# Two transformer blocks on one core: the first attention stage projects its tokens without their root mean square

## The reference, cut to what matters

```python
def rms_norm(x, g):
    y = xf * lax.rsqrt(jnp.mean(xf * xf, axis=-1, keepdims=True) + EPS)     # EPS = 1e-6
    return y * g

h = rms_norm(x, ln_mix[l]);  proj = h @ w_in[l]
q_g, k_g, v_g, q_lat, kv_lat = split(proj)                   # 512, 128, 128, 256, 128 + 32 columns
q_g = apply_rope(rms_norm(q_g per head of 64, gqa_q_norm));  k_g likewise
o_g = attention(q_g, k_g, v_g)                               # 8 heads of 64, 2 key/value heads
c_q = rms_norm(q_lat, mla_q_norm);  c_kv = rms_norm(kv_lat[:128], mla_kv_norm)
k_rope = apply_rope(kv_lat[128:])                            # shared by the 8 latent heads
o_m = attention(c_q @ w_q_b, [c_kv @ w_kv_b, k_rope], values from c_kv @ w_kv_b)
x = x + concat(rms_norm(o_g), rms_norm(o_m)) @ w_o
```

## Time and profile before

| | us |
|---|---|
| median of 3 runs | 3021.49 (3018.26 to 3021.59) |
| the profiled execution, its time | 3016.69 |
| its span, first to last instruction | 3014.9 |
| TensorE busy (matmuls) | 2821.8, 94% of the span |
| VectorE busy | 1422.9, 47% |
| ScalarE busy | 1127.0, 37% |
| GpSimd busy | 238.3, 8% |
| mean granted TensorE clock | 0.974 of full speed |

### The profile page before, as it was taken

How to read it: one execution, slowest core, us unless ns; L and a number is a source line. 1 busy time by engine, 2 the same in 40 slices (tenths; PEclk the granted TensorE clock), 3 DMA queues, 4 the chain that set the end, 5 groups by cost and what they waited for, 6 DMA issues and landing times.

```text
span 3014.9 us, 40098 instructions
## 1 busy us (share of the span) xinstructions
PE 2821.8 (94%) x16212; PEld 2099.0 (70%) x16212; DVE 1422.9 (47%) x2150; ACT 1127.0 (37%) x1917; POOL 238.3 (8%) x229
## 2 busy tenths in 40 slices
PE   7999979989999879999999799999999999799998
PEld 5657844537658744447877578888888787578886
DVE  6665532337666323244545763333334654753444
ACT  4664431124654411135233652222222542643332
POOL 0011020000011100001001010000001111000001
PEclk9999989999999989999999899999999999899999
DMA  4011249981002269983425112233220234222220
GB/s 156 29 43 68 88 175 418 417 356 52 28 29 100 113 254 419 418 354 140 145 99 162 33 72 112 112 120 132 112 84 24 82 120 128 82 84 98 98 98 28
DMA packets 67909, 428.28 MB, mean 142 GB/s; under 512 B 7968, under 2 KB 8352, under 8 KB 20368
## 3 DMA queue, kind: packets, MB, share of 16 engines
q1 hardware_dynamic: 62144, 407.96, 35.4%
q0 software_dynamic: 4432, 15.67, 1.6%
q10 hardware_dynamic: 1152, 2.10, 0.2%
HBM read 416.78 MB, written 8.91 MB: 141 GB/s over the span
## 4 chain that ended last, share of the span: by engine, by line
PE 81%; DVE 7%; ACT 4%; DMA 3%; issue 2%; POOL 2%; SPq 0%; DVEq 0%; ACTq 0%; POOLq 0%
PE banks L854 78%; PE banks L855 3%; ACT arena L1685 3%; DVE arena L2376 3%; DMA weight<-in_w_up 2%; POOL arena L3184 2%; DVE arena L3031 1%; DVE weight_part L2480 1%; ACT weight_part L1685 0%; DVE arena L2665 0%; DVE arena L2663 0%; DMA block_tokens_high<-df_stage 0%; DVE x L2376 0%; DMA weight<-in_ada_w 0%; POOL block_tokens_low L3198 0%
## 5 line engine op out<-in xcount | busy, mean ns | idle before, releaser
L1685 ACT ACTIVATE arena<-banks 128x512 f32<-128x512 f32 (+3 forms) x510 | 279.3, 550 | 876.5 <-PE banks L854 767.5
L854 PE MATMUL banks<-weight,arena 128*64 128x512 f32 (+4 forms) x2136 | 428.9, 573 | 19.1 <-ACT arena L1685 8.5
L854 PE MATMUL banks<-hidden,weight_part 128*128 128x512 f32 (+1 forms) x2304 | 446.8, 355 | 0.0
L854 PEld LDWEIGHTS banks<-hidden,weight_part 128*128 128x128 f32 x2304 | 381.1, 189 | 70.4 <-issue 3.8
L854 PE MATMUL banks<-tokens_high,weight_part 128*128 128x512 f32 (+1 forms) x1536 | 409.6, 358 | 10.0 <-ACT tokens_high L1685 10.0
L2480 DVE TENSOR_TENSOR weight_part<-weight,weight_part 128x2048 fp32r<-128x2048 f32 x124 | 285.6, 2306 | 199.7 <-ACT weight_part L1685 199.6
L1685 ACT ACTIVATE weight_part<-weight 128x2048 fp32r<-128x2048 f32 x124 | 236.4, 1908 | 361.2 <-PE banks L854 336.4
L854 PEld LDWEIGHTS banks<-weight,arena 128*64 128x64 f32 (+2 forms) x2136 | 150.8, 136 | 253.2 <-issue 231.5
L854 PEld LDWEIGHTS banks<-tokens_high,weight_part 128*128 128x128 f32 x1536 | 274.4, 191 | 62.6 <-DVE arena L2376 16.0
L3184 POOL TENSOR_TENSOR arena<-arena 128x512 f32<-128x512 f32 (+1 forms) x89 | 115.9, 1302 | 1978.0 <-ACT arena L1685 1711.4
L854 PE MATMUL banks<-tokens_low,weight_part 128*128 128x512 f32 (+1 forms) x768 | 264.7, 354 | 0.0
(11 more groups left out here) (216 smaller groups left out, 3886.4 us busy)
## 6 DMA issues: line engine op xcount, KB each, us to landing
weight<-in_w_gate SPq DMA_DIRECT2D x64, 1024.0 KB, 13.7
weight<-in_w_up SPq DMA_DIRECT2D x64, 1024.0 KB, 8.1
weight<-in_w_down SPq DMA_DIRECT2D x64, 1024.0 KB, 11.1
weight<-in_w_ff SPq DMA_DIRECT2D x64, 1024.0 KB, 4.8
weight<-in_ada_w SPq DMA_DIRECT2D x48, 1024.0 KB, 6.3
weight<-in_w_in SPq DMA_DIRECT2D x28, 1024.0 KB, 5.9
weight<-in_w_o SPq DMA_DIRECT2D x8, 1024.0 KB, 4.8
weight<-in_w_mem_kv SPq DMA_DIRECT2D x8, 1024.0 KB, 4.9
```

The source lines that it names most:

```text
L854: mm = lambda o, a, b, first=True, last=True: eng.matmul(o, a, b, start=first, stop=last, skip_group_check=True)
L1685: act = lambda o, i, f=ACT.Copy, **k: eng.activation(o, i, f, **k)
```

## The change

HH and HL are made from X * gain, without the root: `tokens_high` (ScalarE, Copy with the gain as scale) and `tokens_low` (VectorE, X * gain - HH). They no longer wait for the squares, which come behind HH in ScalarE's queue. `entry_sums` moves between the high and the low part of `joint3`. All outputs of the projection are now larger by the token's root mean square. Inner norms take that out by themselves, apart from their epsilon: a norm of c/r with EPS is a norm of c with EPS * r * r, r * r being the token's mean square plus EPS. So each sum of squares of g, cq and ckv gets one further matmul (`token_eps`: 64 rows, fp32r, high and low part) that adds EPS * (ms + EPS), and its root and Newton step take epsilon 0. What isn't normed later is scaled by the token's root YM: the values vt and the shared rotated key kr, both now a product on VectorE where ScalarE copied before. The root YM itself (Ln, Exp, Newton) is taken behind the splits of weight chunk 1. On TensorE each per-head sum comes one output later (sum t-2 and turn t-3 follow raw t), and turn 4 comes behind cq 1.

```diff
@@ -607,7 +607,10 @@
             b.update(paired(c, t, T, 4, (2, 2)))
-            b["SQW"] = Ring(st, "SQW" + t, [b["H"][:, k, :] for k in range(KD)])
+            b["SQW"] = Ring(st, "SQW" + t, [Carve((16 + k) * T)(T) for k in range(KD)])
+            b["YM"], b["EPS"] = b["VM"][:, 3, :], b["VM"][:, 0, :]
+            b["EE"] = Carve(35 * T).rounded(f"eps_parts{l}", T)
+            b["EO"] = Carve(36 * T).rounded(f"eps_ones{l}", P)
             B["mix", l] = b
@@ -624,7 +627,7 @@
             b = dict(H=(Carve(0) if l else c)(KD, T), HNH=c.rounded(f"rows_high{l}", TB, D))
-            b["SQW"] = Ring(st, "SQW" + t, [Carve(c.at - (KD - k) * T)(T) for k in range(KD)])
+            b["SQW"] = Ring(st, "SQW" + t, [Carve(c.at - (KD - k) * T if l else (16 + k) * T)(T) for k in range(KD)])
             low_at = c.at
@@ -925,6 +928,23 @@
+            def token_eps(l, o):
+                S = B["mix", l]
+                eng.wait_ge(*after(("ee", l)))
+                return mm(o, S["EO"][0:64, :], S["EE"][0:64, :], False, True)
+            def head_sums(tag, S, nk, ones):
+                l = tag[1]
+                o = PO.take(("ms", tag))
+                if PO.former:
+                    eng.wait_ge(*after(PO.former))
+                for k in range(nk):
+                    eng.wait_ge(*after(("sq", tag, k)))
+                    mm(o, mat(ones), S["SQ"].get((tag, k)), k == 0, False).then_inc(*done(S["SQ"].free((tag, k))))
+                token_eps(l, o).then_inc(*done(("out", ("ms", tag))))
             def norm_sums(tag, S, ks, nk, ones, n=T, ring=PO):
@@ -1009,8 +1029,6 @@
                 H, tag = S["H"], ("mix", l)
-                if l == 0:
-                    entry_sums(tag, S)
                 meet(tag)
@@ -1023,7 +1041,7 @@
                 def gqa_sum(t):
-                    norm_sum(("g", l, t), S, 0, 1, "head64")
+                    head_sums(("g", l, t), S, 1, "head64")
@@ -1031,24 +1049,27 @@
                 joint3([("raw", l, 0), ("raw", l, 1)], [halves(w, 0), halves(w, 1)], HP, [range(KD)], T,
-                       [("hh", tag, k) for k in range(KD)], [("hl", tag, k) for k in range(KD)], [(), (WF(("w_in", l, 0)),)], ("w_in", l, 0))
-                gqa_sum(0)
+                       [("hh", tag, k) for k in range(KD)], [("hl", tag, k) for k in range(KD)], [(), (WF(("w_in", l, 0)),)], ("w_in", l, 0),
+                       between=lambda: entry_sums(tag, B["moe", 0] if l else S))
                 for t in range(2, 5):
                     gqa_raw(t)
-                    gqa_sum(t - 1)
-                    gqa_turn(t - 2)
+                    gqa_sum(t - 2)
+                    if t > 2:
+                        gqa_turn(t - 3)
                 tile3(("vt", l), halves(wcur[0], 1), HP, free=(WF(("w_in", l, 2)),))
+                gqa_sum(3)
+                gqa_turn(2)
+                w = weight_parts(("w_in", l, 3))
+                tile3(("cq", l, 0), halves(w, 0), HP)
                 gqa_sum(4)
                 gqa_turn(3)
-                w = weight_parts(("w_in", l, 3))
-                tile3(("cq", l, 0), halves(w, 0), HP)
-                gqa_turn(4)
                 eng.wait_ge(*after(("vtc", l)))
...
                 tile3(("cq", l, 1), halves(w, 1), HP, free=(WF(("w_in", l, 3)),))
+                gqa_turn(4)
@@ -1084,11 +1105,11 @@
                     if i == 1:
-                        norm_sums(("cq", l), S, range(2), 2, "one256")
+                        head_sums(("cq", l), S, 2, "one256")
                         w = wcur[0] = weight_parts(("w_in", l, 4))
...
                     if i == 2:
-                        norm_sums(("ckv", l), S, range(1), 1, "one128")
+                        head_sums(("ckv", l), S, 1, "one128")
                         tile3(("kr", l), halves(wcur[0], 1), HP, free=(WF(("w_in", l, 4)),))
@@ -1335,7 +1356,8 @@
                         ada(0, 0, k, PO)
-                entry_sums(nxt, NS)
+                if l:
+                    entry_sums(nxt, NS)
@@ -1705,7 +1727,10 @@
                     eng.wait_ge(*after(S["Y"].former))
-                act(y, ring.get(("ms", tag))[:, 0:n], ACT.Ln, bias=eps() if bias is None else bias).then_inc(*done())
+                if tag[0] in ("g", "cq", "ckv"):
+                    act(y, ring.get(("ms", tag))[:, 0:n], ACT.Ln).then_inc(*done())
+                else:
+                    act(y, ring.get(("ms", tag))[:, 0:n], ACT.Ln, bias=eps() if bias is None else bias).then_inc(*done())
                 eng.wait_ge(scalar_step, done.count)
@@ -1778,6 +1803,15 @@
             act(final[:, 0:KD], final[:, 0:KD], ACT.Exp, scale=0.5).then_inc(*done(("final_root",)))
+            def tokens_high(l, ks, needs):
+                for k in ks:
+                    eng.wait_ge(*after(needs(k)))
+                    act(B["mix", l]["HH"][:, k, :], X[:, k, :], ACT.Copy, scale=v1("ln_mix", l, k)).then_inc(*done(("hh", ("mix", l), k)))
+            tokens_high(0, range(4), lambda k: ("xin", k // 2))
+            split_high(("w_in", 0, 0))
+            tokens_high(0, range(4, KD), lambda k: ("xin", k // 2))
             squares(("mix", 0), B["mix", 0], [X[:, k, :] for k in range(KD)], needs=lambda k: ("xin", k // 2))
@@ -1786,16 +1820,19 @@
                     eng.wait_ge(*other)
-                root(tag, S)
-                if l == 0:
-                    split_high(("w_in", 0, 0))
                 def high(t):
...
-                round_tiles([S["HH"][:, k, :] for k in range(KD)], [H[:, k, :] for k in range(KD)], lambda k: ("h", tag, k), lambda k: ("hh", tag, k))
+                eng.wait_ge(*after(("mats",)))
+                act(S["EO"][0:64, :], mat("one1024", 64), scale=32.0).then_inc(*done())
                 split_high(("w_in", l, 1))
                 split_high(("w_in", l, 2))
+                eng.wait_ge(*after(("eps", l)))
+                act(S["EE"][0:64, :], S["EPS"][0:64, :]).then_inc(*done(("eh", l)))
+                act(S["YM"], PO.get(("ms", tag)), ACT.Ln, bias=eps()).then_inc(*done())
+                eng.wait_ge(scalar_step, done.count)
+                act(S["YM"], S["YM"], ACT.Exp, scale=-0.5).then_inc(*done(("y", tag)))
                 for t in range(5):
@@ -1805,7 +1842,6 @@
                         high(t - 2)
-                copy(S["KR"], ("vt", l), PB.get(("vt", l)), ("vtc", l))
                 root(("g", l, 4), S)
@@ -1842,7 +1878,8 @@
                         root(("ckv", l), S)
-                        copy(S["KR"][64:128, :], ("kr", l), PB.get(("kr", l))[64:128, :], ("krc", l))
+                    if i == VM_AT:
+                        eng.wait_ge(*after(("krc", l)))
                     if VM_AT <= i < VM_AT + TB:
@@ -1997,7 +2034,8 @@
                 else:
-                    squares(("mix", 1), S, [X[:, k, :] for k in range(KD)], needs=lambda k: ("x", ("moe", l), k))
+                    tokens_high(1, range(KD), lambda k: ("x", ("moe", 0), k))
+                    squares(("mix", 1), S, [X[:, k, :] for k in range(KD)])
@@ -2411,8 +2449,8 @@
-            def apply(tag, S, src, dst, gains, names, n=T, ring=PO, frees=()):
-                y = rstd(tag, S, ring, n)
+            def apply(tag, S, src, dst, gains, names, n=T, ring=PO, frees=(), eps=EPS):
+                y = rstd(tag, S, ring, n, eps)
                 for k in range(len(src)):
@@ -2491,7 +2529,18 @@
                 H, tag = S["H"], ("mix", l)
-                if l == 0:
+                def tokens_low(ks):
+                    for k in ks:
+                        eng.wait_ge(*after(("hh", tag, k)))
+                        stt(S["HL"][:, k, :], X[:, k, :], v1("ln_mix", l, k), S["HH"][:, k, :], MUL, SUB).then_inc(*done(("hl", tag, k)))
+                if l:
+                    tokens_low(range(KD))
+                else:
+                    tokens_low(range(4))
+                    split_low(("w_in", 0, 0))
+                    tokens_low(range(4, KD))
                     a = S["AC"].get(tag)
@@ -2501,12 +2550,14 @@
                     eng.wait_ge(*other)
-                apply(tag, S, [X[:, k, :] for k in range(KD)], [H[:, k, :] for k in range(KD)], lambda k: v1("ln_mix", l, k), lambda k: (("h", tag, k),))
-                if l == 0:
-                    split_low(("w_in", 0, 0))
-                low_tiles([S["HL"][:, k, :] for k in range(KD)], [H[:, k, :] for k in range(KD)], [S["HH"][:, k, :] for k in range(KD)],
-                          lambda k: ("hh", tag, k), lambda k: ("hl", tag, k))
                 split_low(("w_in", l, 1))
+                eng.wait_ge(*after(("out", ("ms", tag))))
+                m = PO.get(("ms", tag))
+                ts(S["EPS"], m, EPS, EPS, ADD, MUL).then_inc(*done(("eps", l)))
+                eng.wait_ge(*after(("eh", l)))
+                tt(S["EE"][32:64, :], S["EPS"][32:64, :], S["EE"][32:64, :], SUB).then_inc(*done(("ee", l)))
+                eng.wait_ge(*after(("y", tag)))
+                newton(S["YM"], m, S["N"], src_free=(PO.free(("ms", tag)),))
```

(14 more changed lines are left out.)

## The result

The changed kernel takes 3023.6 us (median of 20 runs, 3013.9 to 3029.7); the kernel before, on the same chips, takes 3018.9 (20 runs, 3012.9 to 3024.8). The ratio is 1.0015, with a 95% interval of 1.0008 to 1.0022. So it is slower by 0.15%, some 4.5 us (4.7 between the medians), which lies within the 0.2% that the prediction called no change and inside its range, but on the other side of 1 than the forecast of 1.2 us faster. The profiled execution has a span of 3021.4, against 3014.9.

A forecast was written before the change was run, and what follows sets the result against it. TensorE was taken as the bound (matmuls busy 94% of the span), idling at the mixer's entries. Layer 0 -0.1, layer 1 +1.9 and ckv -0.6 made it 1.2 us faster: 3020.3 us median, range 3011 to 3026.

The forecast's parts named there:

- Entry, layer 0: Mixer entry of layer 0: TensorE starts at 15.05, first outputs done at 30.9 against 35.47, 4.6 us earlier.
- Rival (c): Layer 0 entry: TensorE's clock stays at 0.50 throughout, raw 1 9.8 us later than forecast, kernel 8.6 slower, 3030.1; chance 0.10.
- Entry, layer 1: Mixer entry of layer 1: GpSimd's additions wait for VectorE's low tiles, outputs at 684.7 against 691.28, 6.6 us earlier.
- (a): Layer 1 entry: GpSimd's additions get between VectorE's tiles, layer 1 wins 2.8 us more, 3017.5; chance 0.14.
- From raw 1 to the second scores: Stretch from first outputs to attention: sums one output later, third root 22.2 us after raw 1 instead of 17.0.
- the lag: Lateness after raw 1: 5.2 us, less 0.5 for the vt copy, so 4.7 per layer; 5.7 at upper prices.
- The change leaves these in place: VectorE and ScalarE's chain from third root to second scores (8.95, 6.8, 13.0, 6.6 us) unchanged, except the vt copy.
- Sum: Whole kernel: layer 0 -0.1, layer 1 +1.9, ckv -0.6, so 1.2 us faster.
- All else in both layers follows in TensorE's order: Rest of both layers: expert weight transfers begin when earlier chunks are freed, so shifts pass on; no size added.
- Hidden or small: Small added work: root YM lies under raw 2 (up to 5 us uncovered), kr and cq's epsilon hidden, ckv's epsilon 0.3 per layer.
- The scaling of kr falls in its waits: Attention turn 3: kr's 0.7 us product on VectorE is hidden in VectorE's waits.
- The epsilon for cq runs while VectorE's chain is late: TensorE's epsilon product for cq, ahead of the second scores: hidden, no cost charged.

The follow-up runs named there:

- e10: e5 with layer 1's three additions of squares moved to VectorE behind its eight low tiles, GpSimd idle: 3013.9 us, ratio 0.9976 to the kernel before.
- e4: The changed kernel with the low part of w_o's first chunk moved from ahead of the first maxima to attention turn 5: 3016.4 us, ratio 0.9993.
- e6: The kernel before with only the move of w_o's low part to attention turn 5: 3020.8 us, ratio 1.0007.
- e1: The changed kernel with three unused float32 products filling TensorE's wait behind ckv in each layer: 3021.3 us, ratio 1.0008.
- e3: The kernel before with only the change's later order of per-head sums and turns on TensorE: 3034.7 us, ratio 1.0049.
- e5: e4 with the product that scales kr by YM moved from attention turn 3 to turn 2: 3015.5 us, ratio 0.9993.
- e8: e4 without the epsilon products (token_eps), norms run without the epsilon: 3013.1 us, ratio 0.9984 to the kernel before.
- e9: e5 with both splits of weight chunk 1 moved ahead of the mixer's meeting point: 3010.5 us, ratio 0.9972 to the kernel before.
- e7: e4 with three unused float32 products filling TensorE's wait ahead of the memory norm's sums: 3016.5 us, ratio 0.9993 to the kernel before.

## Why the prediction was wrong, point by point

**Entry, layer 0: right.** 4.9 us earlier (4.6 predicted), first matmul at 14.91 (15). Rival (c) did not come: the first product still runs slow, for 4.4 us where I let it be 4.8 (the last section). I had worked the slow matmuls at 0.427 each; double my own 0.2275 is 0.455, which makes the entry 0.1 longer and rival (c) 1.3 dearer.

**Entry, layer 1: right in size, wrong in its mechanism.** Squares begin 5.8 us earlier (691.51 - 6.02 against 691.28; 6.6 predicted). I had GpSimd wait for the eight tiles because of the 5.47 in the earlier trace rows; it alternated with them, each addition 1.6 to 1.85. The Trainium skill's rule (SBUF — State Buffer, "SBUF: two separate sides"), that the shared ports go to whoever starts first for one whole instruction, agrees with 676.55 to 681.8; e10 shows the other half of it, 3.1 us on VectorE. By that rule alone the addition at 2341 (5.47) should have got in between the tiles as well; why it had to wait is open. Much of what (a) promised was lost again: raw 1 was complete 2.8 earlier than in my forecast, but TensorE then waited 1.26 for chunk 1, and ScalarE, still at the splits, the epsilon parts and the root YM, squared the first output only 3.6 us after it was complete.

**From raw 1 to the second scores: right as a sum.** For entry and lag together I had -0.1 and +1.9 us won; measured are -0.8 and +2.3. In layer 0 the lag was 5.7 (4.7 predicted, with 5.7 as upper end), in layer 1 3.5, since its squares began late. The third norm came 23.1 and 20.9 us behind the squares of the first outputs (22.2 predicted). Of the lag 2.1 was w_o's split, which stood in VectorE's queue in the earlier trace rows at 77.71, and which I passed over in the chain of which I wrote "The change leaves these in place" (e4, e6).

**Sum: the step that failed.** "All else in both layers follows in TensorE's order ... so shifts pass on." They don't pass on unchanged. I had foreseen a wait of 3 us ahead of the second scores, and had counted it as lateness only. It is also idle time, the clock falls in it, and everything behind runs at 1.2 GHz for about 6 us: 2.7 us in each layer of the traces, 5.4 in all (e1, and e3 for the order alone), a term that the sum doesn't have. I had priced the clock at both entries, where TensorE's idle time was shrinking, and not at the one place where the change made it grow. The earlier trace rows with the 5.40 of the earlier trace rows held the warning: 0.60 at 681, behind a wait.

**Hidden or small: two misjudged.** "The scaling of kr falls in its waits": at turn 3 it stands behind two maxima and a copy, and TensorE's fourth scores waited for it, 0.8 per layer (e5). "The epsilon for cq runs while VectorE's chain is late": that product comes behind the wait, not in it, and costs 0.6 per layer (e8); ckv's, which I charged with 0.3, costs nothing.

**The terms again, with measured sizes:** entry and lag 1.5 faster (1.8 predicted, and ckv's 0.6 taken off that), clock 5.4 slower, kr 1.6, cq's epsilon 1.2. Together 6.7 slower by the traces; the times say 4.5, and 6.7 lies just outside their interval of 2.4 to 6.6. One reading would close this gap and those of e1 and e4, all of 2 to 3 us: that the clock doesn't fall behind every wait of 3.1 us, as it did in the two that were traced. The mean granted clock is 0.9757 over the changed kernel's 20 executions, 0.9769 and 0.9768 over the 11 each of e1 and e4. Two falls of 6.8 us at half clock in every execution would make that 0.0023 apart; it is 0.0012, with a standard error of 0.0006. In e3, with waits of 3.9, it is 0.0028 below the kernel before, and there time and trace agree. This is not shown, since only one execution of each kernel was traced. With the moves of e4, e5 and e9 the terms of w_o's split and its clock, of kr and of chunk 1 are gone, and the kernel is 8.5 us faster than the one before. Only the move of w_o's split was also tried in the kernel before (e6).

## What to carry to other kernels

A wait that a change adds on TensorE costs its length and then the clock behind it: where TensorE will stand for 2 us or more, read the granted clock at the nearest wait of that length and charge the slow matmuls until it is back. When a chain gets later, go through the instructions of the engine that carries it and ask of each whether its cover is still there; one weight split moved out of the way was worth twice its length in the traces. A doubtful wait can be tested by filling it with unused products: if the work behind gets faster, it was the clock. Read that from the trace at that place, since here the time alone was too coarse for it.

## What the runs showed of the hardware

A TensorE wait of 2.0 us is at the edge: the same wait, with the same work around it, was followed by the slow level in 11 of 22 passages and by 2.4 GHz in the other 11, at a price of 1.6 us. That the Trainium skill calls the activity window free-running (TensorE: Matmul & The Clock Gate, Part 1) fits, since only the moment differed. At the second scores, waits of 3.1 and 3.9 us led to 0.50 in all four cases (the changed kernel and e3), and waits up to 1.6 us (e8) in none. Such falls are a part of why executions of one kernel differ: over the changed kernel's 20 (3013.9 to 3029.7 us) the mean granted clock runs from 0.979 to 0.973, and the time falls by 2.0 us for each 0.001 of clock (correlation -0.88).

The granted clock's reading is not safe at the start of a program: the windows from 10 to 30 of the changed kernel all show 1.00, while the first 32 matmuls took 9.63 us from 14.91, against 8.08 in layer 1. The reason lies in the trace's clock records: they begin only at 19.34, with a change to 1.00, and where there is no record a window reads 1.00. In the entry of layer 0, TensorE was at the slow level until that first record:

| | first product | first clock record | between | first product to first scores | less half of "between" |
|---|---|---|---|---|---|
| e9 | 16.24 | 19.19 | 2.94 | 59.99 | 58.5 |
| e4 | 15.50 | 18.94 | 3.44 | 60.25 | 58.5 |
| changed kernel | 14.91 | 19.34 | 4.43 | 60.73 | 58.5 |
| e7 | 15.68 | 20.94 | 5.26 | 61.07 | 58.4 |
| e8 | 15.11 | 20.98 | 5.87 | 59.72 | 56.8 |

With half of the slow time taken off, the stretch is 58.4 to 58.5 in all kernels with the changed kernel's order and epsilon products, e1, e5 and e10 too; e8, without the products, stands apart. So stretches that begin at the first product are compared only after this is taken off.
